# Head 0's rotary step moved into the opening; the last head's normalisation, transposes and split moved into the output projection

## What is computed

```python
q, k, v, u = even_project(hs, w_in_even[i])
q = axial_rope(q, rows, cols)
k = axial_rope(k, rows, cols)
k_all = jnp.concatenate([k, cache_attn_k[:, i].astype(k.dtype)], axis=1)
o = diff_attention(q, k_all, v_all, lam)
...
o = rmsnorm(o, subln_g.reshape(ATT_HEADS, ATT_DV)) * (1.0 - lam_init)
p = multiscale_pool(u, w_pool, pool_scale)
return jnp.concatenate([o.reshape(B, T, ATT_WIDTH).astype(p.dtype), p], axis=-1) @ w_out
```

## Time and profile before

| | us |
|---|---|
| median of 3 runs | 2981.57 (2981.26 to 2990.1) |
| the profiled execution, whole | 2987.68 |
| its span in the profile | 2985.8 |
| PE busy in the span | 2770.3 (93%) |
| DVE, ACT, POOL busy | 1298.1, 817.6, 768.3 |
| blocks: opening, attention, trunk of layer 0 begin at | 0, 251.5, 531.1 |

### The profile page before, as it was taken

The page is one execution under the profiler, slowest core; times in us unless marked ns, Lnnn a source line. Parts: engine busy times, 40 slices in busy tenths (PEclk is TensorE's granted clock), DMA queues, the critical chain, the costliest instruction groups (busy, mean ns, idle before and its releaser), DMA issues. The chain is left out here.

```text
span 2985.8 us, 40338 instructions
## 1 busy us (share of the span) xinstructions
PE 2770.3 (93%) x16562; PEld 2645.8 (89%) x16562; DVE 1298.1 (43%) x2121; ACT 817.6 (27%) x1277; POOL 768.3 (26%) x341
## 2 busy tenths in 40 slices
PE   5995888899999999999899996888999999999997
PEld 4994777899999999999899995448999999999996
DVE  5765886673222222222545444554422222222225
ACT  4211666251111111111532222442511111111113
POOL 1553122442111111111322212324321111111112
PEclk9997999899999999999999997998999999999999
DMA  6433100512111111110224335205021111111101
GB/s 239 141 130 86 22 8 1 219 57 87 41 43 41 42 42 42 42 42 32 108 90 161 135 125 202 101 29 219 8 81 42 40 42 42 41 42 42 42 14 64
DMA packets 57436, 226.08 MB, mean 76 GB/s; under 512 B 7344, under 2 KB 17264, under 8 KB 46832
## 3 DMA queue, kind: packets, MB, share of 16 engines
q1 hardware_dynamic: 55744, 224.07, 21.0%
q10 hardware_dynamic: 1584, 0.51, 0.1%
HBM read 190.47 MB, written 29.88 MB: 74 GB/s over the span
## 5 line engine op out<-in xcount | busy, mean ns | idle before, releaser
L216 PE MATMUL ps<-hh,wi_hi 128*128 128x384 f32 x2112 | 707.9, 335 | 0.0
L217 PE MATMUL ps<-hl,wi_hi 128*128 128x384 f32 x2112 | 705.8, 334 | 0.0
L218 PE MATMUL ps<-hh,wi_lo 128*128 128x384 f32 x2112 | 705.8, 334 | 0.0
L1047 DVE TENSOR_TENSOR hid<-ps,hid 128x384 f32<-128x384 f32 x132 | 73.6, 558 | 989.5 <-ACT hid L771 989.5
L216 PEld LDWEIGHTS ps<-hh,wi_hi 128*128 128x128 f32 x2112 | 396.9, 188 | 1.0 <-issue 0.3
L217 PEld LDWEIGHTS ps<-hl,wi_hi 128*128 128x128 f32 x2112 | 396.7, 188 | 1.0 <-issue 0.3
L218 PEld LDWEIGHTS ps<-hh,wi_lo 128*128 128x128 f32 x2112 | 396.7, 188 | 0.0
L771 ACT ACTIVATE hid<-ps 128x384 f32<-128x384 f32 x132 | 65.0, 492 | 1127.9 <-PE ps L218 1127.9
L897 POOL TENSOR_TENSOR wi_lo<-raw_in,wi_hi 128x2048 fp32r<-128x2048 f32 x44 | 203.0, 4614 | 645.5 <-ACT wi_hi L761 645.4
L1058 DVE SCALAR_TENSOR_TENSOR x<-ps,mod,x 128x128 f32<-128x128 f32 (+1 forms) x704 | 327.1, 512 | 76.9 <-PE ps L218 72.7
L216 PE MATMUL ps<-hid_hi,wo_hi 128*128 128x384 f32 x1056 | 354.0, 335 | 2.8 <-DVE x L1058 2.7
(11 more groups left out here) (245 smaller groups left out, 4338.0 us busy)
## 6 DMA issues: line engine op xcount, KB each, us to landing
raw_in<-in_w_ffn_in_dram SPq DMA_DIRECT2D x44, 1024.0 KB, 4.8
wmt<-in_w_mod_t_dram SPq DMA_DIRECT2D x56, 512.0 KB, 3.5
raw_out<-in_w_ffn_out_dram SPq DMA_DIRECT2D x22, 1024.0 KB, 4.8
gla_spill<-turn SPq DMA_DIRECT2D x24, 576.0 KB, 2.8
oraw<-in_w_in_odd_dram SPq DMA_DIRECT2D x24, 512.0 KB, 4.6
wmt_odd<-in_w_mod_t_dram SPq DMA_DIRECT2D x24, 512.0 KB, 5.9
x<-in_x_dram SPq DMA_DIRECT2D x8, 1152.0 KB, 10.5
wm<-in_w_mod_dram SPq DMA_DIRECT2D x16, 512.0 KB, 11.2
```

The lines of the kernel that those rows point to most:

```text
L216: pe.matmul(acc, w_hi, in_hi, start=first, stop=False)
L217: pe.matmul(acc, w_hi, in_lo, start=False, stop=False)
L218: return pe.matmul(acc, w_lo, in_hi, start=False, stop=last)
L1047: dve.tensor_tensor(hid[:, t], ps[:, 2 * t + 1, 0:CW], hid[:, t], ALU.mult).then_inc(hid_done, 1)
```

## The change

**Opening.** SP loads cos, sin and the cached keys during pair 2, and exchanges the partitions of head 0's q in pair 3 and of its k in pair 5. DVE does the rotary step on q behind the modulation tiles of pair 3 and on k behind those of pair 5. The tables lie in the places of the v tiles for that time, so ACT copies tile 12 out only after both steps. A third `recycle` stands between opening and attention.

```diff
+                def turn_head(n):
+                    src = result[:, (Q0, K0)[n]]
+                    sp.wait_ge(taken, NC * ((Q0, K0)[n] + 1))
...
+                    for b in range(8):
+                        to, of = slice(16 * b, 16 * b + 16), slice(16 * (b ^ 1), 16 * (b ^ 1) + 16)
+                        sp.dma_start(turned_qk[n][to, :], src[of, lat]).then_inc(turned_in[n], 16)
...
+                    if p == 2:
+                        sp.wait_ge(rows_done, GROUPS)
+                        for dst, src in ((cos, inp["c_cos"]), (sin, inp["c_sin"])):
...
+                        sp.dma_start(ck[:], inp["cache_k"]).then_inc(ck_in, 16)
+                    elif p == 3:
+                        turn_head(0)
+                    elif p == 5:
+                        turn_head(1)
...
+                    if m == V0:
+                        act.wait_ge(roped, 2)
                     for c in range(NC):
...
+                def rope(n):
...
+                        dve.wait_ge(trig_in, 32)
+                        dve.tensor_scalar(sin[:], sin[:], sgn[:, 0:1], None, ALU.mult).then_inc(signed, 1)
+                    dve.wait_ge(turned_in[n], 128)
...
+                        dve.tensor_scalar(src[:, 0:CTX], src[:, 0:CTX], scale, None, ALU.mult)
...
+                    dve.scalar_tensor_tensor(out=src[:, lat], in0=src[:, lat], scalar=scale, in1=cos[:],
+                                             op0=ALU.mult, op1=ALU.mult).then_inc(rope_part, 1)
+                    dve.scalar_tensor_tensor(out=turned[:], in0=turned[:], scalar=scale, in1=sin[:],
+                                             op0=ALU.mult, op1=ALU.mult).then_inc(rope_part, 1)
+                    dve.wait_ge(rope_part, 2 * n + 2)
+                    dve.tensor_tensor(src[:, lat], src[:, lat], turned[:], ALU.add).then_inc(roped, 1)
...
+                    if p in (3, 5):
+                        rope((p - 3) // 2)
...
+    recycle()
+    even_out = OutWeights("even_out", inp["w_out_even"])
+    last_head = attention(qkvu, WQ, even_out)
+    trunk(0, even_out, inp["x"], lambda kk, cols: (o_hi[kk] if kk < HEADS else p_hi[kk - HEADS])[:, cols],
```

```diff
+                for t in (K0, V0):
+                    name = "new_k" if t == K0 else "new_v"
+                    sp.dma_start(out[name].rearrange("h p t -> p h t"), qkvu[:, t:t + HEADS, 0:CTX]).then_inc(stored, 16)
...
+                    sp.dma_start(dst[:], src).then_inc(trig_in, 16)
+                sp.dma_start(cv[:], inp["cache_v"]).then_inc(cv_in, 16)
+                sp.dma_start(wp[:], inp["w_pool"]).then_inc(wp_in, 16)
...
-                    sp.wait_ge(roped, 2 * h - 1)
+                    need(sp, roped, 2 * h - 3)
                     turn_heads(q_of(h), turned_q, rot_q_in)
-                    sp.wait_ge(roped, 2 * h)
+                    need(sp, roped, 2 * h - 2)
                     turn_heads(k_of(h), turned_k, rot_k_in)
+                sp.wait_ge(roped, 2 * (HEADS - 1))
+                weights.load(sp, 0)
+                weights.load(sp, 1)
...
+                dve.wait_ge(qk_high, 1)
+                dve.tensor_tensor(q_lo[0][:], q_of(0), q_hi[0][:].bitcast(F32), ALU.subtract).then_inc(qk_low, 1)
+                dve.wait_ge(qk_high, 2)
+                dve.tensor_tensor(k_lo[0][:, T:KALL], ck[:, 0], k_hi[0][:, T:KALL].bitcast(F32), ALU.subtract)
+                dve.tensor_tensor(k_lo[0][:, 0:T], k_of(0), k_hi[0][:, 0:T].bitcast(F32), ALU.subtract).then_inc(qk_low, 1)
...
+                    if n == 0:
+                        dve.wait_ge(trig_in, 32)
+                        dve.tensor_scalar(sin[:], sin[:], sgn[:, 0:1], None, ALU.mult).then_inc(signed, 1)
...
+                act.wait_ge(scored, UNITS)
+                weights.cast(act, 0)
...
-                scales(HEADS - 1)
+                weights.split(pool, 0)
```

```diff
+        place = (0, 1, 2, 1, 2, 0, 1, 2)
+        tile_ahead = {3: 1, 4: 2, 5: 0, 6: 3, 7: 4}
...
+        def normalise(self, dve):
+            dve.reciprocal(self.rinv, self.esum).then_inc(self.inverted, 1)
+            dve.wait_ge(self.scale_step, 5)
+            dve.tensor_tensor(self.o_tok[:], self.o_tok[:], self.oscale.unsqueeze(2).broadcast_to([P, NT, P]),
+                              ALU.mult).then_inc(self.normed, 1)
+        def turn(self, pe, b):
+            if b == 0:
+                pe.wait_ge(self.normed, 1)
+            elif b == 2:
+                pe.wait_ge(self.o_low, 1)
+            for j, t in enumerate(self.blocks[b]):
+                mm = pe.transpose(self.bank(b)[:, j * P:(j + 1) * P], self.o_tok[:, t], ident[:])
+            mm.then_inc(self.turned, 1)
...
+        def high(self, act, b):
+            act.wait_ge(self.turned, b + 1)
+            act.activation(o_hi[HEADS - 1][:, self.cols(b)], self.bank(b), ACT.Copy,
+                           scale=subg[:, HEADS - 1:HEADS]).then_inc(self.o_high, 1)
...
+        def low(self, dve, b):
+            dve.wait_ge(self.o_high, b + 1)
+            dve.scalar_tensor_tensor(out=o_lo[HEADS - 1][:, self.cols(b)], in0=self.bank(b), scalar=subg[:, HEADS - 1:HEADS],
+                                     in1=o_hi[HEADS - 1][:, self.cols(b)].bitcast(F32), op0=ALU.mult,
+                                     op1=ALU.subtract).then_inc(self.o_low, 1)
...
+            early = [kk for kk in range(KT) if kk not in late]
             win_in, wout_in = [sem("win_in0"), sem("win_in1")], sem("wout_in")
...
-                        act.wait_ge(multiplied, NC * (m - 2))
-                    act.activation(whi[m % 3][:].rearrange("p k n -> p (k n)"), raw[m % 2][:], ACT.Copy).then_inc(w_high, 1)
...
+                    cast(0)
                 cast(1)
+                if pending is not None:
+                    pending.high(act, 0)
+                    pending.high(act, 1)
                 mods.silu(act)
                 cast(2)
+                if pending is not None:
+                    pending.high(act, 2)
                 for m in range(LAST - 1):
...
-                    pe.wait_ge(w_low, m + 1)
...
-                                     kk == 0, kk == KT - 1)
-                    mm.then_inc(multiplied, 1)
+                    for kk in kks:
+                        mm = product(pe, bank_at(m, c), weights.hi(m)[:, kk], weights.lo(m)[:, kk], in_hi(kk, cs[c]), in_lo(kk, cs[c]),
+                                     kk == 0, kk == kks[-1] and kks is not early)
+                    if kks is not early:
...
-                for m in range(LAST):
+                if pending is not None:
+                    for c in range(NC):
+                        tile(0, c, early)
+                    pending.turn(pe, 0)
+                    pending.turn(pe, 1)
+                    for c in range(NC):
+                        tile(1, c, early)
+                    pending.turn(pe, 2)
+                    for m in range(2):
+                        for c in range(NC):
+                            if m == 0:
+                                pending.ready(pe, c)
...
+                if pending is not None:
+                    pending.normalise(dve)
+                    for b in range(3):
+                        pending.low(dve, b)
+                    dve.wait_ge(pending.o_low, 3)
```

221 lines of the change are left out of this document (124 added, 97 removed).

## The result

| | before | changed |
|---|---|---|
| median of 5 runs, us | 2983.91 (2981.26 to 2990.1) | 2965.22 (2963.03 to 2968.44) |
| the profiled execution | 2987.68 | 2965.08 |
| its span | 2985.8 | 2962.3 |

The ratio is 0.9934, with a 95% interval of 0.9923 to 0.9945: a gain of 18.7 us, and 22.6 between the two profiled executions (23.5 between their spans; 1.9 us of the execution lie outside the span before, 2.8 now). The forecast was 2959 for the median (range 2948 to 2967) and 2965.2 for the profiled execution.

What follows compares the result with a forecast made beforehand. PE waits in holes before attention and the projection, where DVE then sets the pace. 2987.68 - 25.6 + 3.1 = 2965.2 us profiled; the same 22.5 off the median of 2981.57 gives 2959, range 2948 to 2967 (8 in 10).

Steps and rivals of the forecast that it cites:

- Start of attention: Loads and rotary step leave the hole before attention's first scores, which come at 257.4 instead of 283.00: gain 25.6 us.
- Opening: Rotary work and exchanges in the opening cost 0; DVE ends at 248.3, still ahead of PE and ACT (250.7).
- (b): Opening: POOL's additions hold DVE's k step to 11.2 us, so the opening ends 2 to 5 later; 2961 to 2964, chance 0.15.
- End of attention: Between attention and output projection: the first projection product comes at 526.9 instead of 538.14, 11.2 us earlier.
- Projection: Layer 0's output projection: DVE takes its first chunks later and sets the pace; first mean 3.1 us later, a loss.
- The two new waits: PE in the output projection waits 7 us for tile 7's weights and some 9 us at the first mean.
- Layer 1: New buffer order delays ACT's cast of tile 3 some 10 us, but PE needs it 12 us after that: cost 0.
- this lies 6.1 above the median; I subtract the same: Whole kernel: profiled execution is 6.1 above the median of 2981.57; the same 22.5 us subtracted there gives 2959.
- (a): Output projection: the second half's 11.2 us lead is kept because DVE catches up before POOL's chain; 2945, chance 0.12.
- (c): PE's clock stays at full speed into attention, first two units about 3 us shorter; 2956, chance 0.64 together with the forecast.
- (d): Output projection: DVE's pairs slow to 5.9 us (break-even) or more instead of 4.21, kernel slower than before; chance 0.04.
- (e): Start of attention: unit 0 waits for something else of the SP queue, so the hole stays; 2970 to 2981, chance 0.05.

Runs made afterwards that it cites:

- e10: The whole change measured once more with no edit; ratio 0.9931 to the kernel before.
- e7: Whole change plus four modulation tiles ahead of DVE's first taking, x loads spread, POOL's second feed-forward split behind the first mean's sums; 2955.52 us, ratio 0.9892.
- e11: Whole change, but cos, sin and cached keys load behind pair 2's modulation weights instead of ahead; ratio 0.9938 to the kernel before.
- e2: Projection half of the change alone, with the old opening and head 0's rotary step back at attention's start; 2989.96 us against 2985.69 for the kernel before.
- e4: Whole change, but layer 0's output-projection modulation products read 128 of 1024 columns, leaving work out; 2955.57 us, ratio 0.9894 to the kernel before.
- e1: Opening half of the change alone, head 3's scaling, transposes and split back at attention's end, new buffer order kept; 2965.83 us, ratio 0.9935 to the kernel before.
- e5: Opening half alone, with the output weights' three buffers in the old order and places; 2964.22 us, ratio 0.9923 to the kernel before.
- e12: Whole change plus four modulation tiles ahead of DVE's first taking and x loads spread, POOL's order unchanged; 2958.91 us, ratio 0.9909 to the kernel before.

## Why the prediction was right in one place and wrong in another

**Start of attention: right.** 25.6 forecast, 26.1 at the first scores. The working holds step by step: casts and low parts 4.1 us behind the block's start (4.6), DVE's subtraction 1.36 where the product of the earlier trace rows took 1.36. The clearing cost 0.7 instead of 1.35: the block's first instructions start 1.45 us behind the start of the last copy, before the change 0.76. So the two terms of the working were 1.2 us too large together, and the late last copy took back 0.7. **Opening: right** in its cost (0), less so in its margin. The k step took 6.3 us (6.6), but pair 5 began at 190.34 instead of 189.8, pair 6 at 213.20 instead of 211.7, from there to DVE's end it took 1.7 us longer than before the change (38.3 against 36.6), and DVE ended at 251.5 instead of 248.3. Rival (b) would have needed 0.4 us more. In e10 (and, 0.1 us late, in e7) it is there: DVE's last operation begins at 252.40, 0.3 behind the end of ACT's last copy (252.11), and the first scores come 6.0 behind the last copy instead of 5.55.

**End of attention: right.** 11.2 forecast, 11.8 measured: first product 4.5 us behind the last value product, against 16.3. **Projection: right in mechanism and sign, 1.4 too small.** At the third mean the loss is 4.5 instead of 3.1. The other profiles with this projection give 4.0 (e10), 3.7 (e11) and 3.1 (e2, alone with the old opening), so the size is known to about 1 us only. In the first profile the 1.4 come about as follows. Chunk (0,0) was taken at the first product + 26.7, not 25.6. The first product was 0.6 us earlier than forecast behind the last value product, and the three pairs behind the first taking took 9.3, not 10.7, so the fourth taking is 2.3 late and not 3.1. Then one tile more is held: in pair (1,0) a product takes 2.77 us instead of 1.22, since POOL's split of tile 3 runs beside it (at 554.70, before, that split fell into a wait of DVE), and the 13 pairs take 56.2 instead of 54.75. The last part is the clock at the first mean: 1.62 instead of 0.88 us, 0.7 in all, which the prediction had only in its range. The two new waits, 6.6 and 6.1 (in e10 6.5 and 6.4), were forecast at 7 and 9. **Layer 1: 0**, as forecast: its first wait is 1.4 longer, which is the landing of a load (ACT waits 7.9 us for it instead of 6.5); the rest takes 2332.0 against 2331.8. e10 has 2335.1 for the same part, so this zero is good to about 3 us.

**What was missed.** That the parts sum so well to the profiled execution (22.5 against 22.6) is partly luck: attention, with the same work, was 2.2 us shorter, the projection took 1.4 more, and the part outside the span is 0.9 longer. The forecast of the median was 6.2 too low, by the step "this lies 6.1 above the median; I subtract the same". It took the kernel's median from three runs. With five it was 2983.91, and beside the experiments 2984.2 to 2987.3. And it carried over to the changed kernel an offset that is a property of one execution: there the profiled one lies at the median. Of the 6.2 us, 2.3 are the kernel before and 3.8 the gain (18.7 instead of 22.5). The interval of the gain, 16 to 23 us, contains the 22.2 of the two structural terms (26.75 less 4.54), but only just; measured again the change gained 17.1 (e10), and with e11's edit 17.2. What takes back the 3 to 5 us isn't shown. Attention is a candidate: with the new opening it took 236.7 to 241.4 us, 239.0 in the mean of twelve profiles, with the old one 238.9 and 236.8, too few to tell it from chance.

**The rivals.** (a), the lead kept, is refuted, and e4 and e7 show under which condition a good half of it comes true. (b) is refuted for the time, close in the margin: DVE is held, but the three operations of the k step took 1.22, 2.06 and 3.07 us, where (b) wanted some 3.7 each. (c), the clock at full speed into attention, is refuted: in the first 26 us of the scores the granted clock was 0.58 (0.64 in e10, 0.76 in e11), where the kernel before had 0.75, and the first unit's value products end 24.0 us behind the first scores instead of 22.9 (22.4 to 24.1 in the experiments). So nothing was gained there, and in some executions a little lost. (d) is refuted: a pair of DVE took 4.3 us (56.2 / 13), not 5.9. (e) is refuted: in unit 0 DVE waits 1.6 us for the load of sin, but that is covered, since PE's next wait for DVE ends 8.7 us behind the first scores in both kernels.

**What the prediction saw and what it didn't.** It had the second half as a loss of 3.1 us, and measured by itself it is one (e2). It didn't see that the new order of buffers costs 2.7 us to a projection that has no open tiles (e1, e5), nor that four modulation tiles put into DVE's waits turn the loss into a gain (e12, e7). The opening half alone, with the old buffers, is at least as fast as the whole.

## What to carry to other kernels

Starting an engine earlier gains nothing if the engine behind it is the one that sets the pace and starts later: ask at which time the first piece is complete for the next engine, not when the first product begins. Put that engine's side work where it waits anyway, and look for what that work occupies (here PSUM banks and the load queue) before putting in too much of it. Compare two profiles stretch by stretch between events, and leave out a stretch with the same work whose length changes from execution to execution. A median of three and the place of one execution beside it are no basis for a forecast to 6 us.
